# Starting a threshold search earlier, among the gate products, in a two-layer decoder step

## The reference, cut to what matters

```python
# branch A, prompt: keep the best 128 of up to 512 keys; sample: the best 256 of 4097
idx, valid = select_topk(indexer_scores(qi, wi, ki), q_pos, k_pos, topk)
logits = logits + rel_bias[t5_bucket(q_pos - sel_pos)]      # bias by distance, 8 heads
p = softmax(where(valid, logits, -inf));  out = p @ v_sel
# branch B
r = sigmoid(xc @ wa + ba);  i = sigmoid(xc @ wx + bx)       # the gate products
log_a = -8 * r * softplus(-lam);  u = sqrt(-expm1(2 * log_a)) * i * xc
h[t] = exp(log_a[t]) * h[t-1] + u[t];  out = gelu(g) * h
```

## Time and profile before

| | us |
|---|---|
| median of 3 runs | 1349.33 (1347.73 to 1349.34) |
| profiled execution | 1351.15 |
| its span, first to last instruction | 1349.4 |
| PE busy | 1256.8 (93%) |
| PE weight load busy | 1213.2 (90%) |
| DVE busy | 702.3 (52%) |
| ACT busy | 470.2 (35%) |
| POOL busy | 193.0 (14%) |

### The profile page before, as it was taken

One profiled execution on the slowest core, in us unless ns is written; L12 is line 12 of the kernel. 1 busy time (PEld: TensorE's weight loads), 2 busy tenths in 40 slices (PEclk: granted clock), 3 DMA queues, 4 the chain that ended last, 5 costly groups with the idle time before them and its releaser, 6 DMA issues.

```text
span 1349.4 us, 24444 instructions
## 1 busy us (share of the span) xinstructions
PE 1256.8 (93%) x9991; PEld 1213.2 (90%) x9993; DVE 702.3 (52%) x1279; ACT 470.2 (35%) x548; POOL 193.0 (14%) x285
## 2 busy tenths in 40 slices
PE   5998994795999999999999999999999999999995
PEld 5878993563899999999999999999899999999994
DVE  5267786767347555555522244644755555552323
ACT  5243235451224434343322234332543343432110
POOL 0111001106303111111100010030411111110000
PEclk9999997696799999999999999999999999999998
DMA  7143301002222222222222332112122222222211
GB/s 271 64 149 123 132 33 46 1 2 65 68 93 70 89 91 93 93 93 93 87 89 109 102 125 94 64 64 93 63 94 93 93 93 93 93 86 87 86 60 63
DMA packets 25992, 118.17 MB, mean 88 GB/s; under 512 B 7720, under 2 KB 9192, under 8 KB 13904
## 3 DMA queue, kind: packets, MB, share of 16 engines
q1 hardware_dynamic: 21184, 105.50, 22.4%
q0 software_dynamic: 2048, 10.54, 2.3%
q10 hardware_dynamic: 2704, 1.35, 0.4%
HBM read 113.91 MB, written 3.46 MB: 87 GB/s over the span
## 4 chain that ended last, share of the span: by engine, by line
PE 70%; DVE 2%; POOL 1%; ACT 1%; issue 0%; DVEq 0%
PE ps L814 22%; PE ps L815 22%; PE ps L817 22%; POOL xl L1802 1%; PE ps L831 1%; PE ps L950 1%; PE ps L947 1%; PE ps L948 1%; PE ps L1209 0%; DVE acc L1240 0%; DVE vtc L1765 0%; DVE yt L1794 0%; PE ps L1121 0%; DVE rstd L1244 0%; DVE xn L1244 0%
## 5 line engine op out<-in xcount | busy, mean ns | idle before, releaser
L814 PE MATMUL ps<-xh,w_h 128*128 128x260 f32 x1792 | 471.4, 284 | 7.9 <-POOL xl L1802 7.8
L815 PE MATMUL ps<-xl,w_h 128*128 128x260 f32 x1792 | 469.6, 283 | 0.0
L817 PE MATMUL ps<-xh,w_l 128*128 128x260 f32 x1792 | 361.0, 283 | 0.0
L814 PEld LDWEIGHTS ps<-xh,w_h 128*128 128x128 f32 x1792 | 339.4, 189 | 9.1 <-issue 7.6
L815 PEld LDWEIGHTS ps<-xl,w_h 128*128 128x128 f32 x1792 | 338.8, 189 | 0.1
L1233 DVE TENSOR_TENSOR w_l<-w_raw,w_h 128x2048 fp32r<-128x2048 f32 (+1 forms) x94 | 211.6, 2251 | 166.4 <-ACT w_h L503 166.2
L817 PEld LDWEIGHTS ps<-xh,w_l 128*128 128x128 f32 x1792 | 277.1, 189 | 0.0
L815 PE MATMUL ps<-hl,w_h 128*128 128x260 f32 x704 | 183.9, 282 | 0.0
L503 ACT ACTIVATE w_h<-w_raw 128x2048 fp32r<-128x2048 f32 (+1 forms) x50 | 92.3, 1846 | 262.2 <-PE ps L817 242.4
L814 PE MATMUL ps<-hh,w_h 128*128 128x260 f32 x704 | 183.4, 282 | 0.0
L947 PE MATMUL ps<-xh,w_h 128*128 128x260 f32 x448 | 128.9, 309 | 14.1 <-DVE xl L1253 12.5
(11 more groups left out here) (298 smaller groups left out, 1406.3 us busy)
## 6 DMA issues: line engine op xcount, KB each, us to landing
w_raw<-in_wstream SPq DMA_DIRECT2D x86, 1024.0 KB, 4.8
w_raw<-in_wstream SPq DMA_DIRECT2D x8, 768.0 KB, 4.2
res<-in_x_t SPq DMA_DIRECT2D x4, 520.0 KB, 8.3
out_y<-yt SPq DMA_DIRECT2D x8, 260.0 KB, 2.2
tabf<-bias_by_distance SPq DMA_DIRECT2D x1, 2048.0 KB
wm<-in_sgu_w ACTq DMA_DIRECT2D x1, 512.0 KB, 3.6
sb_b<-in_sgu_b ACTq DMA_DIRECT2D x1, 512.0 KB, 4.2
out_f<-ost SPq DMA_DIRECT2D x2, 198.0 KB, 4.6
```

Of the source, the lines that this page charges most:

```text
L814: pe.matmul(out[h], wh, hi[h], start=(first and k == 0), stop=False)
L815: pe.matmul(out[h], wh, lo[h], start=False, stop=False)
L817: ins = pe.matmul(out[h], wl, hi[h], start=False, stop=(last and k == nk - 1))
```

## The change

- **Bias table.** `flip`, `tabf`, `table(m)` and ACT's copies are gone. The scratch is now (8, 128, 640): SP writes `fneg` 128 times after the load of slab 3 and reads the skewed table straight into `tab` in two DMAs after the load of slab 5. `p_logits(0)` waits for them (`d_tabs`). POOL no longer waits for the table, so its first gathers start earlier.
- **Top-k.** The table `rounds` now places all 48 rounds inside `in_ab`.
- **Re-laid scores.** `sc2` lies at `o_relu`; its load waits only for the write to `by_token` and for a memset made in group 5. The loads of `slots` and `relb` come after it.
- **DVE work moved.** `page_columns` runs in group 6 and its second half, `page_terms_out`, after group 9. The transposes of `vt` are at step 12 of group 9 (`turn_values`), the copy to `vn` ahead of `evac_b(9)`.
- **Gates.** Gates 0 and 1 stay after group 9; gates 2 to 7 come one each behind the counts of rounds 0 to 5. `rg_share` moves from rounds 2 to 5 to rounds 7 to 10.
- **Order in a round.** `p_pair` for the next round comes ahead of `p_turn` and `p_values`. POOL's copies `identb` and `pickb` no longer wait for the gates.

```diff
-        tabf = at("tabf", [P, 8, SEQ], F32, o_ik)
-        sc2 = at("sc2", [P, NK], F32, o_wi)
+        sc2 = at("sc2", [P, NK], F32, o_relu)
-        scratch = nc.dram_tensor("bias_by_distance", (8, 640), F32)
+        scratch = nc.dram_tensor("bias_by_distance", (8, P, 640), F32)
@@ SP
-            sp.wait_ge(f_ev, 2)
-            sp.dma_start(scratch.ap(), fneg[:]).then_inc(d_scr, 16)
             for s in range(2, 10):
...
+                if s == 3:
+                    sp.wait_ge(f_ev, 2)
+                    sp.dma_start(scratch.ap(), fneg[:].rearrange("p (a c) -> p a c", a=1).broadcast_to((8, P, 640)))\
+                        .then_inc(d_scr, 16)
+                if s == 5:
                     sp.wait_ge(d_scr, 16)
+                    for h in range(2):
+                        sp.dma_start(tab[:].rearrange("p (j h) c -> p h j c", h=2)[:, h],
+                                     bass.AP(scratch.ap().tensor, 4 * h * P * 640 + P - 1,
+                                             [[639, P], [P * 640, 4], [1, SEQ]])).then_inc(d_tabs, 16)
...
-            sp.wait_ge(b_free, 10)
             sp.wait_ge(col_new, 1)
             sp.wait_ge(d_bytok, 16)
@@ PE
-                if g in (1, 2) and step % 4 == 3:
-                    table(4 * (g - 1) + step // 4)
+                if g == 9 and step == 12:
+                    turn_values()
-            for n in range(8):
+            def gate(n):
+            gate(0)
+            gate(1)
             def p_work(rnd):
+                for i in heads(rnd + 1):
+                    if i % 2 == 0:
+                        p_pair(i // 2)
                 for i in heads(rnd - 1):
                     p_turn(i)
...
             for rnd in range(32):
                 count(rnd)
+                if rnd < 6:
+                    gate(rnd + 2)
+                if rnd == 7:
+                    pe.wait_ge(sig_done, 8)
                 p_work(rnd)
@@ DVE
-            rounds = {4: (0, 0, 3), 5: (4, 4, 2), 6: (4, 4, 2), 7: (4, 4, 2), 8: (0, 0, 0), 9: (4, 5, 0)}
+            rounds = {4: (0, 0, 4), 5: (4, 6, 2), 6: (4, 5, 2), 7: (4, 6, 3), 8: (0, 0, 1), 9: (4, 3, 0)}
+                if g == 9:
+                    dve.wait_ge(vn_tr, 1)
+                    dve.wait_ge(d_kvi, 48)
+                    dve.tensor_copy(vn[:].rearrange("p n c -> p (n c)"), ps[:, 4, :]).then_inc(vn_ev, 1)
                 evac_b(g)
+                if g == 6:
+                    page_columns()
-            page_columns()
-            topk_rounds(q, 3 * ROUNDS - q)
+            page_terms_out()
-                if 2 <= rnd < 6:
-                    rg_share(rnd - 2)
+                if 7 <= rnd < 11:
+                    rg_share(rnd - 7)
@@ POOL
-            pool.wait_ge(tab_ev, 8)
-            pool.wait_ge(gate_mm, 8)
```

More of the change, by code:

```diff
@@ L88, in build_step @@
     (wstream, x_t, vec, rg_w, h0, conv0, ffn0, pages, page2, cache_kv, cache_i, rel, rel4, sgu_w, sgu_b,
-     sgu_w0, sgu_b0, c_ident, c_flip, c_dist, c_blocks, c_pick, c_slots) = ins
+     sgu_w0, sgu_b0, c_ident, c_dist, c_blocks, c_pick, c_slots) = ins
     y_o, k_o, v_o, ki_o, h_o, c_o, cv_o, f_o = outs
@@ L175, in build_step @@
         fneg = at("fneg", [8, 640], F32, o_gg + 2560)
-        flip = at("flip", [P, P], F32, o_gg + 5120)
         relt = at("relt", [32, 8], F32, o_gg + 5632)
         blocks = at("blocks", [P, 2, P], F32, o_gg + 5696)
-        tabf = at("tabf", [P, 8, SEQ], F32, o_ik)
         rr, ii, th = (at(n, [P, 4, T], F32, o_xn + 8320 * i) for i, n in enumerate(("rr", "ii", "th")))
@@ L292, in build_step @@
         d_st, hst_done, ap_mm = sem("d_st"), sem("hst_done"), sem("ap_mm")
-        d_flip = sem("d_flip")
+        d_tabs = sem("bias_table")
         d_wax, d_rgs, d_pt = sem("d_wax"), sem("d_rgs"), sem("d_pt")
@@ L298, in build_step @@
         setup_v = sem("setup_v")
-        f_mm, f_ev, tab_mm, tab_ev = sem("f_mm"), sem("f_ev"), sem("tab_mm"), sem("tab_ev")
+        f_mm, f_ev = sem("f_mm"), sem("f_ev")
         wi_tr, wi_nat, idx_mm, relu_done, score_acc, causal, topk_done = (
@@ L353, in grp @@
             return ps[:, 4 * parity + 2 * tile:4 * parity + 2 * tile + 2, 0:HT]
-        def head_of(m):
-            return m // 2 + 4 * (m % 2)
         FILL = {"in_ab": 0, "out_ab": 1, "up0": 2, "in_c": 3, "out_c": 4, "up1": 5}
@@ L414, in _ @@
             load(1, 1)
-            for dst, src, done in ((flip, c_flip, d_flip), (pt, pages, d_pt), (pg2, page2, d_const),
+            for dst, src, done in ((pt, pages, d_pt), (pg2, page2, d_const),
                                    (blocks, c_blocks, d_const), (picks, c_pick, d_const), (h0s, h0, d_rgs)):
                 sp.dma_start(dst[:], src).then_inc(done, 16)
-            sp.wait_ge(f_ev, 2)
-            sp.dma_start(scratch.ap(), fneg[:]).then_inc(d_scr, 16)
             for s in range(2, 10):
@@ L423, in _ @@
                 load(s, s % 2)
-                if s == 2:
+                if s == 3:
[3 more added lines that the diff above has]
+                if s == 5:
                     sp.wait_ge(d_scr, 16)
-                    sp.dma_start(tabf[:], bass.AP(scratch.ap().tensor, 0, [[1, P], [640, 8], [1, SEQ]])).then_inc(d_scr, 16)
+                    for h in range(2):
+                        sp.dma_start(tab[:].rearrange("p (j h) c -> p h j c", h=2)[:, h],
+                                     bass.AP(scratch.ap().tensor, 4 * h * P * 640 + P - 1,
+                                             [[639, P], [P * 640, 4], [1, SEQ]])).then_inc(d_tabs, 16)
                 if s == 7:
@@ L438, in _ @@
             sp.dma_start(bass.AP(by_token.ap().tensor, 0, [[NT, P], [NT * P, DEC], [1, NT]]), sc[:]).then_inc(d_bytok, 16)
-            sp.wait_ge(slab_done, 10)
-            sp.dma_start(slots[:], c_slots).then_inc(d_late, 16)
-            sp.dma_start(relb[:], rel4).then_inc(d_late, 16)
-            sp.wait_ge(b_free, 10)
             sp.wait_ge(col_new, 1)
@@ L448, in _ @@
                          allow_slow_non_contiguous=True).then_inc(d_sc2, 16)
+            sp.wait_ge(slab_done, 10)
+            sp.dma_start(slots[:], c_slots).then_inc(d_late, 16)
+            sp.dma_start(relb[:], rel4).then_inc(d_late, 16)
             sp.wait_ge(w_hi, 10)
@@ L541, in gelu_of @@
                 act.activation(gg[:, 2 * g - 15, :], gg[:, 2 * g - 15, :], ACT.Gelu_apprx_tanh).then_inc(gelu_b, 1)
-            def table(m):
-                act.wait_ge(tab_mm, m + 1)
-                act.activation(tab[:, m, :], ps[:, 4 + m % 2, :], ACT.Copy).then_inc(tab_ev, 1)
             def relu(i):
@@ L839, in bias_products @@
                 pe.matmul(ps[0:8, 5, 0:128], relt[:], dist[:, 512:640], start=True, stop=True).then_inc(f_mm, 1)
[L841 to L847, removed]
             def turn_weights():
-                pe.wait_ge(tab_ev, 8)
                 pe.wait_ge(d_c, 16)
@@ L930, in beside, with turn_values @@
                         score_unit(u - 1)
+                if g == 9 and step == 12:
+                    turn_values()
+            def turn_values():
+                pe.wait_ge(ev_a, NUNITS_I - 1)
+                for n in range(NCH):
+                    ins = pe.transpose(ps[:, 4, n * P:(n + 1) * P], vt[:, n * P:(n + 1) * P], ident[:])
+                ins.then_inc(vn_tr, 1)
             def by_tiles(s, a_ready, b_ready, beside, g, x_wait=None):
@@ L1040, in p_work @@
                         p_out(blk)
-                for i in heads(rnd + 1):
-                    if i % 2 == 0:
-                        p_pair(i // 2)
             for rnd in range(32):
                 count(rnd)
+                if rnd < 6:
+                    gate(rnd + 2)
+                if rnd == 7:
+                    pe.wait_ge(sig_done, 8)
                 p_work(rnd)
@@ L1398, in page_columns, with page_terms_out @@
                 ch.link(ts(pgc[:, 1, :], pgf[:, 1, :], float(P), None, ALU.mult))
+            def page_terms_out():
                 dve.tensor_copy(ptab[:, NK:NK + 1], col("chunk", 0))
@@ L1432, in _ @@
                     decay_constants()
+                    dve.memset(sc2[:, 2 * P:NK], OUT).then_inc(col_new, 1)
                 if g == 8:
@@ L1452, in _ @@
             dve.wait_ge(b_free, 10)
-            dve.memset(sc2[:, 2 * P:NK], OUT).then_inc(col_new, 1)
             dve.memset(zero1, 0.0)
@@ L1456, in _ @@
             ch.link(dve.memset(quart1, 16384.0))
-            dve.wait_ge(vn_tr, 1)
-            dve.wait_ge(d_kvi, 48)
-            dve.tensor_copy(vn[:].rearrange("p n c -> p (n c)"), ps[:, 2, :]).then_inc(vn_ev, 1)
-            page_columns()
-            topk_rounds(q, 3 * ROUNDS - q)
+            page_terms_out()
+            assert q == 3 * ROUNDS
             dve.wait_ge(pstep, 2)
@@ L1528, in p_logits @@
                 blk, m, nk = i // 8, i % 8, P * (i // 8 + 1)
+                if i == 0:
+                    dve.wait_ge(d_tabs, 32)
                 dve.wait_ge(qk_done, i + 1)
@@ L1950, in shape_constants @@
```

(6 more changed lines are left out.)

## The result

The changed kernel takes 1374.94 us (median of four runs, 1372.64 to 1376.13) beside 1348.53 for the kernel before: ratio 1.0196, 95% interval 1.0176 to 1.0216. It is slower where 11 us less were forecast. The profiled execution took 1372.64 us (span 1370.9).

What follows compares the result with a forecast made beforehand. PE (70% of the span) was taken to bound the kernel, a serial DVE chain its 220 to 240 us. -7.0 + 1.0 + 1.6 - 20.0 + 13.4 = -11.0 us gave 1338.3 us; own range 1334 to 1343, overall 1329 to 1346.5.

Steps and rivals of the forecast that it cites:

- I take the slab rate ... and so 0 exposed: Scratch table write behind slab 3: 12.0 us at the slab rate, ending near 38, 0 exposed; upper bound 198 us.
- rival (d): Scratch write from eight partitions holds slab 4 in SP's queue, costing above 25 us; at 45 us, 1358 us; chance 0.06.
- Rounds 11 on. I put 0: Bisection rounds from 11 on with p_pair first: 0 us, from -2 to +1, as PE does the same work each round.
- Table, -7.0: Groups 1 and 2: eight table-product steps leave PE, 0.87 us each, -7.0 us.
- Group 4 to 5, +1.0: PE's wait for ACT's copy behind slab 6's split, 3.87 us already, grows by 1.0 us; bounds 0 and +3.
- Groups 6 to 8, +1.6: Added rounds and page_columns (1.0 us taken) make PE start group 9 later by 1.6 us.
- Start, -20.0: From PE's end of group 8 to the bisection's first count: 28.8 us instead of 48.8, so -20.0 us.
- Rounds 0 to 10, +13.4: First count to comparison 11: 26.3 us instead of 12.9, with gates behind counts and ACT's chain exposed; +13.4 us.

Runs made afterwards that it cites:

- experiment 1: Changed kernel with the scratch write issued by ACT on its own queue behind the first norm's root, instead of by SP: 1343.70 us, ratio 0.9977 to the kernel before.
- experiment 3: Changed kernel with the same scratch write issued from 128 partitions instead of 8: 1344.18 us, ratio 0.9974; from 16 partitions, a single execution: 1349.01 us.
- experiment 5: Kernel before with the table part of the change alone, its write from 128 partitions: 1344.84 us beside 1351.67, ratio 0.9953.
- experiment 2: Kernel before with every part of the change except the table (old flip and table products kept): 1351.28 us, ratio 1.0024.
- experiment 6: Experiment 4's kernel with six gates instead of two ahead of the first count: 1331.99 us, ratio 0.9861 to the kernel before.
- experiment 8: Experiment 7's kernel with ACT's square root moved behind the last transposed head, and two idle products in round 10: 1328.54 us, ratio 0.9850 to the kernel before.
- experiment 4: Experiment 1's kernel with p_work in its old order (p_pair of the next round last): 1336.38 us, ratio 0.9918 to the kernel before.
- experiment 7: Experiment 6's kernel plus PE products that nothing reads, behind the counts of rounds 2 to 10: 1328.34 us, ratio 0.9834 to the kernel before.

## Why the prediction was wrong

- **The step that failed: the table's "I take the slab rate ... and so 0 exposed".** The write took 55.9 us where 12.0 was taken, and slab 4 behind it cost 25.8 us of stall and some 3.3 of half clock. The rival (d) named this mechanism, its place and its price (at 45 us: 19.7 late), and the bounds 12 and 198 held the value; it got a chance of 0.06. (By its arithmetic a write of 55.9 us makes slab 4 30.6 late; the split came 27.2 after 55.8.) The two bounds came from writes or loads that were unlike it (a load into 128 partitions; 20 KB with its fixed cost), and the nearer-looking one was taken. By the Trainium skill (DMA: Bandwidth & Descriptors, "Why a DMA increments its semaphore by 16 and not by 1") a slowest dimension of eight on both sides means eight of 16 engines; the traces agree (a share of 0.46, and 0.93 with a dimension of 16). But the prediction gave those engines the slab's speed (24 us), and the write took 2.3 times as long.
- **Second, smaller: "Rounds 11 on. I put 0".** +9.1 in the changed kernel, +5.8 and +7.5 in experiments 1 and 3, -0.2 with the old order. The reason given, that PE does the same work whatever its order, holds for the work; what it left out is the clock at which PE does it. Half clock for 31.5, 24.2 and 27.7 us, for 10.8 before, accounts for these sizes.
- **Table, -7.0:** right; 6.4 us by the ratio and 7.6 at the first comparison in experiment 5.
- **Group 4 to 5, +1.0:** the wait is as forecast (4.85 us, 3.87 before). What follows was not: from PE's restart to the next split it took 0.8 us longer than before in the changed kernel's profiled execution and 3.1 to 3.5 in experiments 1 to 3, since the clock stayed at half for longer. With the wait that is 1.8 and 4.1 to 4.5 us, in the experiments above the prediction's upper bound of 3. (With the old pause, in experiment 5, nothing was lost.) Of experiment 3, the wait and two windows from there on:

```profile
100.91 1.68 PE L887 MATMUL ps<-qibd,ikt 128*128 128x16 f32 x8 [4.85 <-ACT ikt L555]
...
100.00:104.00 4.00, 3.09 (x15) 3.09 (x16) 3.14 (x18) 1.33 (x4) 0.00 (x0) 0.65 0.63 250
104.00:108.00 4.00, 4.00 (x21) 4.00 (x20) 2.07 (x7) 0.60 (x1) 0.00 (x0) 0.50 0.00 0
```

- **Groups 6 to 8, +1.6:** PE waits 1.3 to 1.4 us before group 9, and `page_columns` takes 0.7 us for the 1.0 taken. Right, but for what follows the wait.
- **Start, -20.0:** in experiment 3 PE waits until 187.68 before group 9, 1.35 of it, and the first comparison is at 216.12; with 0.55 from there to the count that is 30.3 us from PE's end of group 8, for 30.4 forecast (28.8 + 1.6). Right in sum, but by luck, since two errors cancel. The scores landed 1.4 earlier than taken (2.9 us for 4.3). And group 9's first half, up to `evac_a(9)`, took 12.0 us for 10.2: behind the pause of 1.35 us the clock was 0.50 from 190 to 192 us and 0.67 from 192 to 194, a term that the prediction put at nothing. Of experiment 3:

```profile
199.69 0.70 DVE L1275 TENSOR_TENSOR gg<-ps,rstd 128x520 f32<-128x520 f32 x1 [3.16 <-PE ps L941]
...
216.12 0.49 DVE L1493 SCALAR_TENSOR_TENSOR cmpb<-ps,sm 128x257 bf16<-128x257 f32 x1
```

- **Rounds 0 to 10, +13.4:** +11.5. The six counts behind gates took 8.3 us for 10, since the clock rose midway; both DVE waits (4.73 and 4.42) came where they were named, and experiments 6 and 8 show that ACT's chain is the cause.

Up to `gt` the profiled execution adds up: -11.0 forecast, +29.1 for the slab, +9.1 in rounds 11 on and -1.9 in rounds 0 to 10 make 25.3, for 25.5 measured. The 4.0 us less from there to the end lie within the scatter of that part (last section).

With the table fixed and nothing else, the change is worth 3 to 4 us (experiments 1 and 3), not 11: the difference is the longer half clock in rounds 11 on, which comes with the order in the round, and in group 5.

## What to carry to other kernels

Price a DMA by a row with the same source and destination layout, not by its bytes: count the partitions it reads and the packets on each engine, and ask what is queued behind it before asking what waits for its data. Before moving an instruction to the front of an engine's queue, list what then stands behind it, and read the granted clock as well as the waits afterwards: here the order cost 6 us while PE was busy nearly all the time. A shorter chain pays only as far as the engines behind it are free: in experiment 8 a lead of 3.9 us at `gt` was 0.2 at the first gather.

## What the runs showed of the hardware

- A write of 1,024 rows of 2,560 bytes took 55.9 us from 8 partitions, 31.0 from 16 and 16.4 from 128, at DMA shares of 0.46 and 0.93 for the first two. A busy share near full says nothing of the rate: 102 GB/s at 0.93 from 16 partitions, 413 at 1.01 with the write from 128 and a slab beside it.
- The same slow write on ACT's queue held half of the engines' share and made two 1,024 KB slabs on SP's queue land after 20.9 and 13.2 us (median of the page 4.8), in time for PE; ahead of slab 4 on SP's own queue it made that slab land after 48.8.
- A pause of PE of the same 4.85 us was followed by half clock for about 7 us in the profiled execution of the changed kernel and for about 10 in that of experiment 3 (worked out from windows of 2 us; 1.6 of the 7 still lie in the pause). A pause of 1.35 us before group 9 of experiment 3 was followed by some 3.4 us of it.
- A busy PE is not a PE at full clock: 19.61 of 20 us busy at 0.50 in experiment 1, 19.62 at 0.74 in experiment 4.
- DVE operations on 1 to 4 columns took 1.07 to 1.25 us beside elementwise products on POOL (four in `page_columns` of the kernel before, two in experiment 8) and 0.15 to 0.17 without them (changed kernel, experiment 7); others beside the same products were not slowed.
- What lies between `gt` and the end took 1045.3 to 1045.8 us in four profiled executions and 1048.8 to 1050.6 in seven, whatever the edit (experiment 8, with its gathers, left out). At the same distance from `gt`, the clock is 0.84 from 330 to 340 us in experiment 3 (1045.3) and 0.50 from 327 to 337 in experiment 1 (1050.6). Single profiles of these kernels can't be compared to better than these 5 us.
